# Banded attention on one Trainium2 core: two head pairs per round instead of one

## The chip, the cores and the metric

The kernel runs on one core of a Trainium2 chip. The metric is the device time of one execution in microseconds (us). The engines of the core work side by side: TensorE (PE in the rows, its weight loads PEld), VectorE (DVE), ScalarE (ACT), GpSimd (POOL), and SyncE (SP), which here only issues DMAs. Each engine runs its own instructions in order and waits on semaphores for the others.

## The reference, cut to what matters

Two blocks follow each other on 1024 tokens of width 1024. The second has three mixers; the change touches the third, attention within a band, and the order of the products that run beside it.

```python
def mixer_window_attention(q, k, v, gate, sink, bias, mask):
    # 8 query heads of 64, 2 key/value heads (4 query heads share one), blocks of 128 queries;
    # each block sees its own 128 keys, the 128 before and the 128 after
    s = jnp.einsum('bnqkgd,bnskd->bnkgqs', q, kb).astype(jnp.float32) * (HEAD_DIM_2 ** -0.5)
    s = jnp.where(mask[None, :, None, None], s + bias, NEG_INF_2)
    m = jnp.maximum(jnp.max(s, axis=-1, keepdims=True), sk)
    p = jnp.exp(s - m)
    p = p / (jnp.sum(p, axis=-1, keepdims=True) + jnp.exp(sk - m))
    o = jnp.einsum('bnkgqs,bnskd->bnqkgd', p.astype(vb.dtype), vb)
    return o.reshape(bsz, seq, W_C) * jax.nn.silu(gate)
# after the mixers: y = concat(ya, yb, yc) @ w_out;  x = layer_norm(ALPHA * x + y, ...)
```

## The kernel before, in words

All engines have programs written out by hand; nothing but the order of the calls and the semaphores sets the order of the work. The last stage but one is attention. Its unit is a **pair** `x` of 0 to 31 (`pair`, L362): two query heads of one block of 128 queries, `g` the key/value head (0 for x < 16), `n` the block, `p` which two of the four heads; `nb` is the number of key blocks in the band, 3, and 2 at both ends of the sequence (x = 0, 1, 14, 15, 16, 17, 30, 31).

Four kinds of work go to TensorE, each with its own shape in the array:

- `pair_scores(x)` (L1212, **S**): queries times keys, both heads at once in the two row halves of the array (64 rows by 128 columns), `nb*128` columns, into one bank of PSUM per head, banks 0 and 1. In the trace these are four records of L1220.
- `turn_p(x)` (L1223, **T**): `2*nb` transposes of the weights in the full array, banks 4 and 5, L1229.
- `weigh(x)` (L1233, **W**): the value products, the two heads in the two column halves (128 by 64), `4*nb` records of L1240, bank 6 or 7.
- `side(n, ks)` (L1244): a piece of one of the dense products that fill the time, in the full array with 512 columns each, three matmuls per step of k (L841, L842, L843), banks 2 and 3. For x < 16 a round takes three steps of k (9 matmuls; gates and queries of g = 1), for x >= 16 a whole tile of four steps (12 matmuls; the first half of the output product).

The loop at L1277 issues per round x: W(x-1), T(x), S(x+2), side. After it come 16 tiles of the output product (`tail`, L1291), with W(31) behind the first.

The other engines follow a pair in this way. DVE adds bias and takes the minimum of the negated scores (`pair_scores`, L1859, one custom instruction per head, L1869, into `sp[:, x % 2]`, which must have been transposed for x-2). ACT makes the exponentials and their sums in place (`weights`, L2346, L2352). DVE takes the reciprocal (`row_scale`, L1873), POOL multiplies both heads' rows by it (`scale_p`, L782, L787), TensorE transposes. ACT copies head 0 of the transposed weights out of bank 4 (`turned`, L2355, L2360), DVE head 1 out of bank 5 (`turned`, L1887, L1892), into the one buffer `pT`, which W(x-1) must have read. After W(x), DVE multiplies the product by the gate (`gate_out`, L1877, L1885). Between these stand on DVE and ACT the ends of the side products (`side_out`, dictionary `SIDE_OUT`, L375; for x >= 17 DVE adds the residual to the tile of the round before, L1907), and at `PIECE` (L373) the splitting of finished output features into a high and a low part (`high_y2` on ACT, L2310, `low_y2` on DVE, L1799). POOL also splits the coming weights into high and low parts, a quarter at a time (`split_part`, L762, L768 and L771): the first `W_Q1`, then the four chunks `W_O2` to `W_O2+3`. SP loads chunk `W_O2+3` (L600) when chunk `W_O2+2` has been split, and POOL splits it when side product 23 has left its buffers.

In PSUM a bank is taken with `take(b, name, value)` (L818): it waits for the semaphore that the bank's last user named.

```python
            for x in range(32):
                if x:
                    weigh(x - 1)
                if x == 16:
                    pe.wait_ge(s["v_y2lo"], 8)
                turn_p(x)
                if x + 2 < 32:
                    pair_scores(x + 2)
```

Of the kernel before, what the change touches and what calls it, by code (L numbers as in the profile page):

```python
# [7 lines left out]
F32 = mybir.dt.float32  # L8
# [98 lines left out]
def build(nc, I, out):  # L107
# [64 lines left out]
    with ctx:  # L172
# [3 lines left out]
        def region(kb4, *groups):  # L176

            found = []
            for group in groups:
                with ExitStack() as tmp:  # L180
                    found += [tmp.enter_context(nc.sbuf_tensor(n, s, t)) for n, s, t in group]
            sb(f"pad_{groups[0][0][0]}", [P, kb4])
            return found

        def sem(name):
# [4 lines left out]
        whi = [sb(f"whi{i}", [P, KT, CW], F32R) for i in range(2)]  # L190
        wlo = [sb(f"wlo{i}", [P, KT, CW], F32R) for i in range(2)]
        SL = KT * S
        (u_hi, u_lo, qT0, qT1, kt0, kt1, v0, v1, ST0, ST1, Wb, yt1, tmpj, smzb, h2, Q, y2a, _q, y2b, glu, _h, agb) = region(
            2 * SL,
            [("u_hi", [P, KT, S], F32R), ("u_lo", [P, KT, S], F32R)],
            [("qT0", [P, 2, S], F32), ("qT1", [P, 2, S], F32),
# [7 lines left out]
            [("y2a", [P, 4, 2, S], F32R), ("_q", [P, 2, NT * CW], F32), ("y2b", [P, 2, 2, S], F32R)],  # L204

            [("glu", [P, 2, GPAD], F32), ("_h", [P, 6 * S - 2 * GPAD - 4], F32), ("agb", [P, 2, S], F32)],
        )
        xr, yp_hi, um, ym_hi, x2_hi, res = region(
            SL, [("xr", [P, NT, D], F32)], [("yp_hi", [P, KT, S], F32R)], [("um", [P, KT, S], F32)],
            [("ym_hi", [P, KT, S], F32R)], [("x2_hi", [P, KT, S], F32R)], [("res", [P, NT, D], F32)])  # L210
        yp_lo, cc, ym_lo, x2_lo, y2c = region(
            SL, [("yp_lo", [P, KT, S], F32R)], [("cc", [P, KT, S], F32)],
            [("ym_lo", [P, KT, S], F32R)], [("x2_lo", [P, KT, S], F32R)], [("y2c", [P, 2, 2, S], F32R)])
        qTs, kts, vs, STs = (qT0, qT1), (kt0, kt1), (v0, v1), (ST0, ST1)

        pxhi, pxlo = yp_hi[:, 6:8, :], yp_lo[:, 6:8, :]
# [151 lines left out]
        def piece(i):  # L368

            g, hf, p = i // 4, i % 4 // 2, i % 2  # L370
            return g, hf, p, 16 * g + 8 * hf + 6 + p

        PIECE = {piece(i)[3] + 1: i for i in range(8)}  # L373

        SIDE_OUT = {0: 1, 3: 2, 6: 3, 8: 4, 11: 5, 14: 6, 16: 7}  # L375
        SIDE_OUT.update({17 + t: 8 + t for t in range(2 * NT)})
# [438 lines left out]
        def _(pe):  # L815
            last = {}

            def take(b, name, value):  # L818

                if b in last:  # L820
                    pe.wait_ge(s[last[b][0]], last[b][1])
                last[b] = (name, value)
                bank_of[name, value] = b
                return bank[b]
# [387 lines left out]
            def pair_scores(x):  # L1212
                g, n, p, lo, nb = pair(x)
                if x in (0, 1, 16, 17, 24, 25):
                    pe.wait_ge(s["a_q"], {0: 4, 1: 4, 16: 5, 17: 6, 24: 7, 25: 8}[x])
                for i in range(2):
                    ko = 64 * i
                    keys = kA if i == g else kB
                    ps = take(i, "v_s", 2 * x + i + 1)
                    pe.matmul(ps[:, 0:nb * P], qT2[ko:ko + 64, p, n * P:(n + 1) * P],  # L1220
                              keys[ko:ko + 64, lo * P:(lo + nb) * P], start=True, stop=True).then_inc(s["t_sc"], 1)

            def turn_p(x):  # L1223
                _, _, _, _, nb = pair(x)
                for i in range(2):
                    pe.wait_ge(s["g_nm"], 2 * x + i + 1)
                    ps = take(4 + i, ("a_pT", "v_pT")[i], x + 1)
                    for b in range(nb):
                        mm = pe.transpose(ps[:, b * P:(b + 1) * P],  # L1229
                                          sp[:, x % 2, i, BAND - (nb - b) * P:BAND - (nb - b - 1) * P], idn)  # L1230
                    mm.then_inc(s["t_pt"], 1)

            def weigh(x):  # L1233
                g, _, _, lo, nb = pair(x)
                ps = take(6 + x % 2, "v_o", x + 1)
                pe.wait_ge(s["a_pT"], x + 1)
                pe.wait_ge(s["v_pT"], x + 1)
                for b in range(nb):
                    for i in range(2):
                        mm = pe.matmul(ps[64 * i:64 * i + 64, 0:P], vt[:, lo + b, g * HD2:(g + 1) * HD2],  # L1240
                                       pT[:, i, b * P:(b + 1) * P], start=(b == 0), stop=(b == nb - 1))
                mm.then_inc(s["t_pv"], 1)

            def side(n, ks=range(KT)):  # L1244

                b = 2 + n % 2
                if n < 4:
                    w, i, name, value, hi, lo = W_CG1, n, "v_cg", n + 1, x2_hi, x2_lo
                elif n < 8:
                    w, i, name, value, hi, lo = W_Q1, n - 4, "a_q", n + 1, x2_hi, x2_lo  # L1250
                else:
                    w, i, name, value, hi, lo = W_O2 + (n - 8) // NT, n % NT, "v_r2", n - 7, y2_hi, y2_lo
                if ks[0] == 0:
                    side_bank[n] = take(b, name, value)
                group(w, i, hi, lo, name, value, ks=ks, ps=side_bank[n])
# [18 lines left out]
            side(0)  # L1274
            pair_scores(1)
            side(1)
            for x in range(32):  # L1277
                if x:
                    weigh(x - 1)
                if x == 16:  # L1280
                    pe.wait_ge(s["v_y2lo"], 8)
                turn_p(x)
                if x + 2 < 32:
                    pair_scores(x + 2)
                if x < 16:
                    for k in range(3 * x, 3 * x + 3):
                        side(2 + k // KT, range(k % KT, k % KT + 1))
                else:
                    side(8 + x - 16)

            def tail(i):  # L1291
                c, t = TAIL[i]
# [5 lines left out]

            for i in range(len(TAIL)):
                tail(i)  # L1300
                if i == 0:
                    weigh(31)

        def filled(eng, t_name, t_value, name, value):

# [5 lines left out]
        def _(ve):  # L1311
# [547 lines left out]
            def pair_scores(x):  # L1859
                g, n, p, _, nb = pair(x)  # L1860
                off = P if n == 0 else 0
                if n == 0:
                    ve.wait_ge(s[f"l_rb{p}"], 32 * (g + 1))
                for i in range(2):
                    ps = filled(ve, "t_sc", 2 * x + i + 1, "v_s", 2 * x + i + 1)
                    if x >= 2:
                        ve.wait_ge(s["t_pt"], 2 * x + i - 3)
                    h = 4 * g + 2 * p + i
                    ve.tensor_tensor_reduce(sp[:, x % 2, i, BAND - nb * P:BAND], ps[:, 0:nb * P],  # L1869
                                            rbias[:, 2 * p + i, off:off + nb * P], 1.0, nsink[:, h:h + 1],  # L1870
                                            ALU.add, ALU.min, nm[:, x % 2, i:i + 1]).then_inc(s["v_s"], 1)

            def row_scale(x):  # L1873
                ve.wait_ge(s["a_p"], 2 * x + 2)
                ve.reciprocal(rcx[:, x % 2, :], smx[:, x % 2, :]).then_inc(s["v_rc"], 1)  # L1875

            def gate_out(x):  # L1877
                g, n, p, _, _ = pair(x)
                if x == 0:
                    ve.wait_ge(s["a_f"], 12)  # L1880
                if x == 16:
                    ve.wait_ge(s["v_cg"], 4)
                ps = filled(ve, "t_pv", x + 1, "v_o", x + 1)
                y = gated[g][:, p, n * P:(n + 1) * P]
                ve.tensor_tensor(y, ps[:, 0:P], y, ALU.mult).then_inc(s["v_o"], 1)  # L1885

            def turned(x):  # L1887
                nb = pair(x)[4]
                ps = filled(ve, "t_pt", 2 * x + 2, "v_pT", x + 1)
                if x:  # L1890
                    ve.wait_ge(s["t_pv"], x)
                ve.tensor_copy(pT[:, 1, 0:nb * P], ps[:, 0:nb * P]).then_inc(s["v_pT"], 1)  # L1892

            def side_out(n):

# [23 lines left out]
            side_out(0)  # L1919
            for n in range(4, 8):  # L1920
                low_y2(n)
            for x in range(33):
                if x + 1 < 32:
                    row_scale(x + 1)
                if x:
                    gate_out(x - 1)
                if x < 32:
                    turned(x)
                if x + 2 < 32:
                    pair_scores(x + 2)  # L1930
                if x in SIDE_OUT:
                    side_out(SIDE_OUT[x])
                if x in PIECE:
                    low_y2(8 + PIECE[x])

            def final_norm(t):

# [31 lines left out]
        def _(ac):  # L1969
# [385 lines left out]
            def turned(x):  # L2355
                nb = pair(x)[4]
                ps = filled(ac, "t_pt", 2 * x + 1, "a_pT", x + 1)
                if x:
                    ac.wait_ge(s["t_pv"], x)
                ac.activation(pT[:, 0, 0:nb * P], ps[:, 0:nb * P], ACT.Copy).then_inc(s["a_pT"], 1)  # L2360

            def side_out(n):

# [14 lines left out]
            for x in range(33):  # L2378
                if x < 32:
                    turned(x)  # L2380
                if x in SIDE_OUT:
                    side_out(SIDE_OUT[x])
                if x + 2 < 32:
                    weights(x + 2)
                if x in PIECE:
                    high_y2(8 + PIECE[x])
            for t in range(NT):
                ac.wait_ge(s["v_lnv"], NH + NT + 2 + t + 1)
                root(sd[:, t:t + 1], v1_[:, t:t + 1])
# [29 lines left out]
```

## Time and profile before

| | |
|---|---|
| median of 3 runs | 1217.81 us (1216.48 to 1218.27) |
| the profiled execution's own time | 1219.74 us |
| its span in the trace | 1217.7 us |
| TensorE busy | 1183.7 us, 97% of the span |
| VectorE, GpSimd, ScalarE busy | 684.5, 450.1, 357.1 us |
| granted clock of TensorE, mean | 0.993 |

The span is the stretch that the trace covers, from the first instruction to the last; the own time has some 2 us around it. "Busy" counts the time in which an engine has an instruction in work. Start times in rows are us from the start of the span. Matmuls are pipelined, so that the records of neighbours overlap: the distance from one start to the next is what a matmul costs, and not its duration.

### The profile page before, as it was taken

The numbers are of one execution on the slowest core, as the hardware profiler recorded it, in microseconds if no ns is written. First come the engines' busy times: TensorE is split into PE (matmuls) and PEld (weight loads), VectorE is DVE, ScalarE is ACT, GpSimd is POOL, SyncE is SP. The second block draws the span as 40 slices with busy tenths as digits, with TensorE's granted clock in tenths as the row PEclk, the third lists the DMA queues.
The fourth block names the chain that finished last, engine by engine and source line by source line (L and its number), as shares of the span: only waits on it lengthen the run. The fifth ranks groups of instructions, "written<-read, shape, count | busy, mean of one in ns | idle before, by whom it ended". The sixth has DMA issues, their size and how long they took to land.

```text
span 1217.7 us, 15892 instructions
## 1 busy us (share of the span) xinstructions
PE 1183.7 (97%) x5921; PEld 953.9 (78%) x5921; DVE 684.5 (56%) x1242; ACT 357.1 (29%) x714; POOL 450.1 (37%) x431
## 2 busy tenths in 40 slices
PE   6999999999999999999998999999999999999995
PEld 5788888888888688787786788879888886666784
DVE  4545647342476303167767946856794524555468
ACT  6312121000012102546565511331111144443211
POOL 3324222232522322445665664203422315444343
PEclk9999999999999999999999999999999999999998
DMA  7141121453221222101114412232121110051102
GB/s 231 38 145 44 35 78 35 132 176 101 70 69 35 70 95 105 44 23 28 52 40 147 165 52 70 87 100 70 53 69 35 62 35 35 9 191 36 50 39 121
DMA packets 73884, 93.47 MB, mean 77 GB/s; under 512 B 13905, under 2 KB 53033, under 8 KB 73298
## 3 DMA queue, kind: packets, MB, share of 16 engines
q1 hardware_dynamic: 65090, 88.27, 21.6%
q10 hardware_dynamic: 8720, 4.20, 1.3%
q8 instruction: 48, 0.79, 0.3%
q14 instruction: 26, 0.21, 0.1%
HBM read 75.11 MB, written 18.92 MB: 77 GB/s over the span
## 4 chain that ended last, share of the span: by engine, by line
PE 86%; DVE 7%; POOL 2%; issue 2%; DMA 1%; ACT 1%; SPq 0%; ACTq 0%; POOLq 0%; DVEq 0%
PE bank L841 22%; PE bank L843 21%; PE bank L842 21%; PE bank L1066 3%; PE bank L1083 3%; PE bank L1220 2%; PE wide L1240 2%; PE wide L1229 2%; PE wide L1076 2%; DVE res L1943 1%; PE bank L1037 1%; PE bank L1026 1%; PE wide L841 1%; PE wide L843 1%; PE wide L842 1%
## 5 line engine op out<-in xcount | busy, mean ns | idle before, releaser
L622 POOL CAST whi<-wraw 128x2048 fp32r<-128x2048 f32 x31 | 58.9, 1900 | 463.1 <-PE bank L843 394.2
L841 PE MATMUL bank<-u_hi,wlo 128*128 128x512 f32 x512 | 201.2, 393 | 3.3 <-DVE u_lo L1338 3.3
L843 PE MATMUL bank<-u_hi,whi 128*128 128x512 f32 x512 | 199.8, 390 | 0.0
L842 PE MATMUL bank<-u_lo,whi 128*128 128x512 f32 x512 | 199.7, 390 | 0.0
L624 POOL TENSOR_TENSOR wlo<-wraw,whi 128x2048 fp32r<-128x2048 f32 x32 | 153.1, 4784 | 3.0 <-ACT whi L2252 0.5
L841 PE MATMUL bank<-x_hi,wlo 128*128 128x512 f32 x320 | 128.1, 400 | 0.8 <-issue 0.7
L843 PE MATMUL bank<-x_hi,whi 128*128 128x512 f32 x320 | 124.8, 390 | 0.0
L842 PE MATMUL bank<-x_lo,whi 128*128 128x512 f32 x320 | 124.8, 390 | 0.0
L841 PEld LDWEIGHTS bank<-u_hi,wlo 128*128 128x128 f32 x512 | 96.5, 189 | 25.6 <-DVE u_lo L1338 4.4
L843 PEld LDWEIGHTS bank<-u_hi,whi 128*128 128x128 f32 x512 | 96.4, 188 | 20.4
L842 PEld LDWEIGHTS bank<-u_lo,whi 128*128 128x128 f32 x512 | 96.6, 189 | 19.5
L841 PEld LDWEIGHTS bank<-x_hi,wlo 128*128 128x128 f32 x320 | 60.1, 188 | 21.7 <-issue 9.7
L787 POOL TENSOR_SCALAR sp<-sp,rcx 128x384 f32<-128x384 f32 (+1 forms) x64 | 36.1, 577 | 105.9 <-DVE rcx L1875 105.9
L843 PEld LDWEIGHTS bank<-x_hi,whi 128*128 128x128 f32 x320 | 60.1, 188 | 12.9
L1788 DVE SCALAR_TENSOR_TENSOR wide<-glu,VT,wide 128x1024 f32<-128x1024 f32 x58 | 69.3, 1280 | 0.0
L842 PEld LDWEIGHTS bank<-x_lo,whi 128*128 128x128 f32 x320 | 60.1, 188 | 11.4
L1083 PE MATMUL bank<-v,kwb 128*128 128x257 f32 x224 | 59.0, 386 | 1.1 <-DVE Cst L1588 0.9
L1066 PE MATMUL bank<-Cst,qT 128*128 128x257 f32 x224 | 58.1, 381 | 0.9 <-ACT tmpj L2174 0.8
L1465 DVE SCALAR_TENSOR_TENSOR cva<-um,VT,cva 128x1022 f32<-128x1022 f32 (+1 forms) x32 | 58.0, 1811 | 1.1
L2056 ACT ACTIVATE um<-bank 128x512 f32<-128x512 f32 x16 | 9.6, 599 | 155.7 <-PE bank L843 155.7
L710 POOL TENSOR_TENSOR Pm<-ST,Wb 128x128 f32<-128x128 f32 x64 | 30.3, 473 | 60.5 <-ACT Wb L2126 60.5
L1869 DVE CUSTOM_DVE_ANT_0 sp<-bank,rbias,nsink 128x384 f32<-128x384 f32 (+1 forms) x64 | 34.9, 582 | 29.4 <-PE bank L1220 29.1
(335 smaller groups left out, 2420.0 us busy)
## 6 DMA issues: line engine op xcount, KB each, us to landing
wraw<-in_w_in SPq DMA_DIRECT2D x27, 1024.0 KB, 5.3
wraw<-in_w_out SPq DMA_DIRECT2D x12, 1024.0 KB, 5.1
xr<-in_x SPq DMA_DIRECT2D x8, 512.0 KB, 8.4
hst<-in_x SPq DMA_DIRECT2D x4, 1024.0 KB, 5.1
hpool<-hst SPq DMA_DIRECT2D x4, 1024.0 KB, 4.1
smz<-mzs SPq DMA_DIRECT2D x16, 256.0 KB, 2.1
wraw<-nmax ACTq DMA_DIRECT2D x32, 128.0 KB, 3.0
h<-hpool SPq DMA_DIRECT2D x4, 1024.0 KB, 6.4
```

The costliest lines, as they stand in the source:

```text
L622: g_.tensor_copy(whi[w % 2][:, :, :], wraw[:, :, :]).then_inc(s["w_hi"], 1)
L624: g_.tensor_tensor(wlo[w % 2][:, :, :], wraw[:, :, :], whi[w % 2][:, :, :].bitcast(F32), ALU.subtract).then_inc(s["w_lo"], 1)
L710: g_.tensor_tensor(Pm[:, n % 2, :], STs[h % 2][:, ck, :], Wb[:, n % 2, :], ALU.mult).then_inc(s["g_P"], 1)
L787: g_.tensor_scalar(row, row, rcx[:, x % 2, i:i + 1], 0.5 if g else 1.0, ALU.mult, ALU.mult).then_inc(s["g_nm"], 1)
L841: pe.matmul(ps, al, bh, start=(k == 0), stop=False)
L842: pe.matmul(ps, ah, bl, start=False, stop=False)
L843: return pe.matmul(ps, ah, bh, start=False, stop=(k == nk - 1))
L1066: mm = pe.matmul(ps[:, 0:AUG], q[:, k, ck * P:(ck + 1) * P], Cst[:, d, k, :], start=(k == 0), stop=(k == 1))
L1083: mm = pe.matmul(ps[:, 0:AUG], kwb[:, m % 2, k * P:(k + 1) * P], v[:, ck, :], start=True, stop=True)
L1465: ins = ve.scalar_tensor_tensor(acc[:, a0:a1], um[:, j, a0 + sh:a1 + sh], tap(q), acc[:, a0:a1], ALU.mult, ALU.add)
L1788: ins = ve.scalar_tensor_tensor(dst, src, w, acc, ALU.mult, ALU.add)
L1869: ve.tensor_tensor_reduce(sp[:, x % 2, i, BAND - nb * P:BAND], ps[:, 0:nb * P], rbias[:, 2 * p + i, off:off + nb * P], 1.0, nsink[:, h:h + 1],
```

## The change

TensorE takes two pairs per round. With x0 even, a round is W(x0-2), W(x0-1), S(x0+2), S(x0+3), then T(x0) with its side products and T(x0+1) with its side products. W(30) and W(31) stand behind the last side product and ahead of the first tail tile. Every instruction stays what it was, in shape and number.

Banks are dealt out anew: S takes 0 and 1 for even x and 6 and 7 for odd x, W takes 4 (even) or 5 (odd), which T uses too. The transposed weights get a second buffer: even x use `pT`, odd x use `pTb` (x < 16) or `pTc`, which lie in parts of other regions that are free then, so that a copy of `turned(x)` waits for W(x-2) and no more for W(x-1). DVE's order becomes, per x0: `gate_out(x0-2)`, `gate_out(x0-1)`, `row_scale(x0+1)`, `turned(x0)`, `pair_scores(x0+2)`, `side_out(x0)`, two `low_y2` at x0 = 8, 16, 24, 32, `turned(x0+1)`, `row_scale(x0+2)`, `pair_scores(x0+3)`, `side_out(x0+1)`. ACT keeps its order, but for the two `high_y2`, which move. POOL and SP are unchanged.

```diff
+            [("_b", [P, 2 * SL - 2 * S], F32), ("pTb", [P, 2, S], F32)],
...
+            [("_c", [P, 2 * S], F32), ("pTc", [P, 2, S], F32)])
...
-        PIECE = {piece(i)[3] + 1: i for i in range(8)}
+        PIECES = {piece(i)[3] + 2: (i, i + 1) for i in range(0, 8, 2)}
+
+        def pT_of(x, i):
+            if x % 2 == 0:
+                return pT[:, i, :]
+            return (pTb if x < 16 else pTc)[:, i, HALF:HALF + BAND]
...
-                    ps = take(i, "v_s", 2 * x + i + 1)
+                    ps = take(6 * (x % 2) + i, "v_s", 2 * x + i + 1)
...
-                ps = take(6 + x % 2, "v_o", x + 1)
+                ps = take(4 + x % 2, "v_o", x + 1)
...
-                                       pT[:, i, b * P:(b + 1) * P], start=(b == 0), stop=(b == nb - 1))
+                                       pT_of(x, i)[:, b * P:(b + 1) * P], start=(b == 0), stop=(b == nb - 1))
...
-            for x in range(32):
-                if x:
-                    weigh(x - 1)
-                if x == 16:
+            for x0 in range(0, 32, 2):
+                if x0:
+                    weigh(x0 - 2)
+                    weigh(x0 - 1)
+                if x0 + 2 < 32:
+                    pair_scores(x0 + 2)
+                    pair_scores(x0 + 3)
+                if x0 == 16:
                     pe.wait_ge(s["v_y2lo"], 8)
-                turn_p(x)
-                if x + 2 < 32:
-                    pair_scores(x + 2)
-                if x < 16:
-                    for k in range(3 * x, 3 * x + 3):
-                        side(2 + k // KT, range(k % KT, k % KT + 1))
-                else:
-                    side(8 + x - 16)
+                for x in (x0, x0 + 1):
+                    turn_p(x)
+                    if x < 16:
+                        for k in range(3 * x, 3 * x + 3):
+                            side(2 + k // KT, range(k % KT, k % KT + 1))
+                    else:
+                        side(8 + x - 16)
+            weigh(30)
+            weigh(31)
...
             for i in range(len(TAIL)):
                 tail(i)
-                if i == 0:
-                    weigh(31)
...
-                if x:
-                    ve.wait_ge(s["t_pv"], x)
-                ve.tensor_copy(pT[:, 1, 0:nb * P], ps[:, 0:nb * P]).then_inc(s["v_pT"], 1)
+                if x >= 2:
+                    ve.wait_ge(s["t_pv"], x - 1)
+                ve.tensor_copy(pT_of(x, 1)[:, 0:nb * P], ps[:, 0:nb * P]).then_inc(s["v_pT"], 1)
...
-            for x in range(33):
-                if x + 1 < 32:
-                    row_scale(x + 1)
-                if x:
-                    gate_out(x - 1)
-                if x < 32:
-                    turned(x)
-                if x + 2 < 32:
-                    pair_scores(x + 2)
-                if x in SIDE_OUT:
-                    side_out(SIDE_OUT[x])
-                if x in PIECE:
-                    low_y2(8 + PIECE[x])
+            for x0 in range(0, 34, 2):
+                if x0:
+                    gate_out(x0 - 2)
+                    gate_out(x0 - 1)
+                if x0 < 32:
+                    row_scale(x0 + 1)
+                    turned(x0)
+                if x0 + 2 < 32:
+                    pair_scores(x0 + 2)
+                if x0 in SIDE_OUT:
+                    side_out(SIDE_OUT[x0])
+                for i in PIECES.get(x0, ()):
+                    low_y2(8 + i)
+                if x0 < 32:
+                    turned(x0 + 1)
+                if x0 + 2 < 32:
+                    row_scale(x0 + 2)
+                    pair_scores(x0 + 3)
+                if x0 + 1 in SIDE_OUT:
+                    side_out(SIDE_OUT[x0 + 1])
...
-                if x:
-                    ac.wait_ge(s["t_pv"], x)
-                ac.activation(pT[:, 0, 0:nb * P], ps[:, 0:nb * P], ACT.Copy).then_inc(s["a_pT"], 1)
+                if x >= 2:
+                    ac.wait_ge(s["t_pv"], x - 1)
+                ac.activation(pT_of(x, 0)[:, 0:nb * P], ps[:, 0:nb * P], ACT.Copy).then_inc(s["a_pT"], 1)
...
+                for i in PIECES.get(x, ()):
+                    high_y2(8 + i)
                 if x in SIDE_OUT:
                     side_out(SIDE_OUT[x])
                 if x + 2 < 32:
                     weights(x + 2)
-                if x in PIECE:
-                    high_y2(8 + PIECE[x])
```

## Rows read from the trace of the kernel before

**Rows 1.** The page: shares of the chain of waits that ended last, by engine.
```profile
PE 86%; DVE 7%; POOL 2%; issue 2%; DMA 1%; ACT 1%; SPq 0%; ACTq 0%; POOLq 0%; DVEq 0%
```

**Rows 2.** Busy time in stretches of attention; last come granted clock, DMA share, GB/s.
```profile
1005.40:1080.00 74.60, 74.60 (x482) 50.06 (x481) 37.07 (x120) 32.94 (x91) 34.34 (x67) 1.00 0.13 43
1080.00:1164.00 84.00, 84.00 (x519) 59.48 (x520) 42.28 (x121) 27.30 (x76) 35.40 (x60) 1.00 0.23 86
```

**Rows 3.** Timeline of TensorE, one round of x >= 16: start, duration, line, tiles.
```profile
1098.35 0.88 PE L1240 MATMUL wide<-pT,vt 128*64 128x128 f32 x12
1099.16 0.88 PE L1229 MATMUL wide<-cst,sp 128*128 128x128 f32 x6
1099.96 0.59 PE L1220 MATMUL bank<-kB,qT 64*128 64x384 f32 x1
...
1100.81 0.50 PE L841 MATMUL bank<-whi,y2a 128*128 128x512 f32 x1
1101.15 0.40 PE L842 MATMUL bank<-wlo,y2a 128*128 128x512 f32 x1
...
1103.43 0.39 PE L843 MATMUL bank<-whi,y2a 128*128 128x512 f32 x1
1103.75 0.88 PE L1240 MATMUL wide<-pT,vt 128*64 128x128 f32 x12
```

**Rows 4.** Timeline of TensorE, the same kinds in other neighbourhoods and sizes.
```profile
979.90 0.40 PE L843 MATMUL bank<-x_hi,whi 128*128 128x512 f32 x1
980.13 1.91 PE L1269 MATMUL wide<-cst,Q 128*128 128x128 f32 x16
981.80 0.47 PE L841 MATMUL bank<-x_hi,wlo 128*128 128x512 f32 x1
982.11 0.39 PE L842 MATMUL bank<-x_lo,whi 128*128 128x512 f32 x1
...
992.90 0.48 PE L1220 MATMUL bank<-kA,qT 64*128 64x256 f32 x1
...
993.22 0.38 PE L1220 MATMUL bank<-kA,qT 64*128 64x256 f32 x1
...
993.53 0.50 PE L841 MATMUL bank<-x_hi,wlo 128*128 128x512 f32 x1
...
1156.10 0.66 PE L1240 MATMUL wide<-pT,vt 128*64 128x128 f32 x8
1156.69 0.66 PE L1229 MATMUL wide<-cst,sp 128*128 128x128 f32 x4
1157.10 0.47 PE L841 MATMUL bank<-whi,y2a 128*128 128x512 f32 x1
```

**Rows 5.** Groups by line in 993 to 1170: busy, mean ns, idle before, releaser.
```profile
L2352 ACT ACTIVATE sp<-sp,nm 128x385 f32<-128x385 f32 x48 | 29.3, 614 | 30.6 <-DVE nm L1869 30.6
L1869 DVE CUSTOM_DVE_ANT_0 sp<-bank,rbias,nsink 128x384 f32<-128x384 f32 x48 | 27.7, 616 | 7.3 <-PE bank L1220 7.3
L787 POOL TENSOR_SCALAR sp<-sp,rcx 128x384 f32<-128x384 f32 x48 | 27.6, 588 | 65.3 <-DVE rcx L1875 65.3
...
L1892 DVE COPY pT<-wide 128x384 f32<-128x384 f32 x24 | 13.4, 558 | 11.8 <-PE wide L1229 11.8
...
L1907 DVE SCALAR_TENSOR_TENSOR res<-res,bank 128x512 f32<-128x512 f32 x16 | 10.9, 682 | 0.0
...
L1885 DVE TENSOR_TENSOR Q<-wide,Q 128x128 f32<-128x128 f32 x32 | 9.3, 290 | 36.8 <-PE wide L1240 36.8
```

**Rows 6.** Timelines of POOL, SP and DVE from the last pair into the tail.
```profile
1152.67 1.28 POOL L771 TENSOR_TENSOR wlo<-wraw,whi 128x512 fp32r<-128x512 f32 x1
1160.25 0.61 POOL L768 CAST whi<-wraw 128x512 fp32r<-128x512 f32 x1 [6.29 <-PE bank L843]
...
1153.98 0.38 SPq L395 DMA_DIRECT2D wraw<-in_w_out  x1
...
1179.51 3.13 DVE L1943 SCALAR_TENSOR_TENSOR res<-res,mv,pog 128x1024 f32<-128x1024 f32 x1
```

More of the change, by code:

```diff
@@ L192, in build @@
         SL = KT * S
-        (u_hi, u_lo, qT0, qT1, kt0, kt1, v0, v1, ST0, ST1, Wb, yt1, tmpj, smzb, h2, Q, y2a, _q, y2b, glu, _h, agb) = region(
+        (u_hi, u_lo, qT0, qT1, kt0, kt1, v0, v1, ST0, ST1, Wb, yt1, tmpj, smzb, h2, Q, y2a, _q, y2b, glu, _h, agb, _b, pTb) = region(
             2 * SL,
@@ L210, in build @@
             [("ym_hi", [P, KT, S], F32R)], [("x2_hi", [P, KT, S], F32R)], [("res", [P, NT, D], F32)])
-        yp_lo, cc, ym_lo, x2_lo, y2c = region(
+        yp_lo, cc, ym_lo, x2_lo, y2c, _c, pTc = region(
             SL, [("yp_lo", [P, KT, S], F32R)], [("cc", [P, KT, S], F32)],
-            [("ym_lo", [P, KT, S], F32R)], [("x2_lo", [P, KT, S], F32R)], [("y2c", [P, 2, 2, S], F32R)])
+            [("ym_lo", [P, KT, S], F32R)], [("x2_lo", [P, KT, S], F32R)], [("y2c", [P, 2, 2, S], F32R)],
+            [("_c", [P, 2 * S], F32), ("pTc", [P, 2, S], F32)])
         qTs, kts, vs, STs = (qT0, qT1), (kt0, kt1), (v0, v1), (ST0, ST1)
```

## The prediction, made before the change was run

> **What bounds the kernel now.** I read the page first. TensorE is busy for 97% of the span, and the chain of waits that ended last runs through it for 86% and through VectorE for 7% [rows 1]. Next the table of stretches: in attention TensorE is busy for all of 1005.4 to 1080 and of 1080 to 1164, at the full granted clock (1.00, the 2.4 GHz level), while DVE is at half, ACT at 30 to 45%, POOL at 45% [rows 2]. TensorE never runs dry there, so no engine or DMA beside it can give time back; only its own instruction stream can get shorter. The change removes no instruction. The question is therefore what TensorE pays where one kind of work follows another, and the timeline of TensorE shows that in the distances between starts.
>
> Within a side product matmuls start every 0.228 us (1101.15 to 1103.43 are ten) [rows 3]. Around the other kinds it takes longer. Bare lengths follow from two sizes of each: W takes 0.59 with 8 records and 0.81 with 12, so 0.22 per key block and 0.81 - 3 x 0.213 = 0.17 beside it; the six transposes of T before S take 0.80, sixteen alone take 1.67 (0.104 each), so 0.17 beside 0.63; S with 256 columns takes 0.63 and with 384 columns 0.85, so 0.21 beside 0.64 [rows 3, 4]. Of these 0.21, 0.11 lie between S's own two passes (0.32 apart at 256 columns, bare 0.21) and 0.10 behind it. The first side matmul after S takes 0.34 for 0.23 (0.11 more), and the last before W 0.32 for 0.23 (0.09 more) [rows 3]. So a round pays, beside bare work: side to W 0.09, W to T 0.17, T to S 0.17, inside S 0.11, S to side 0.21, in all 0.75 us of 5.40.
>
> What of this is a matter of changing the array's division? T and side both use the whole array: side to T costs 0.23 for 0.23 (979.90 to 980.13), nothing; T to side costs no gap (four transposes 0.41) and 0.08 on the first matmul (0.31 at 981.80) [rows 4]. These are the two neighbourhoods that the new order has instead.
>
> **The change, part by part.** Two rounds now hold eight borders: 1.50 us. Afterwards a double round has W W S S T side T side:
>
> - side to W 0.09, as now [rows 3].
> - W to W: same division, two banks. Not in the trace; nearest are the twelve records inside one W, which have no gap, and W to T at 0.17. I take 0, range 0 to 0.17.
> - W to S: from column halves to row halves, not in the trace; W to T and T to S both cost 0.17, side to W only 0.09. I take 0.17, range 0.09 to 0.21.
> - inside S and S to S: the first S has its 0.11; the second S may load its weights behind the first, so I take 0.05 for it, range 0 to 0.21 (0.11 inside it and 0.10 between them).
> - S to T: S to side costs 0.10 ahead of the first matmul and 0.11 on it; T's first load has its price in T to side. I take 0.10, range 0.05 to 0.21.
> - side to T 0, range 0 to 0.09; T to side 0.08, twice [rows 4], range 0.04 to 0.08.
>
> Sum 0.09 + 0 + 0.17 + 0.11 + 0.05 + 0.10 + 0 + 0.16 = 0.68, saved 1.50 - 0.68 = 0.82 us per double round. There are 14 full ones (x0 = 2 to 28): 11.5 us. The first (x = 0 and 1, no W of an earlier pair) had T to S twice, S twice, S to side twice, side to W and W to T, 1.24; it gets side to S 0.09, S 0.16, S to T 0.10 and T to side 0.16, 0.51: saved 0.7. The last (x = 30, 31 and W(31)) had side to W three times, W to T twice, T to side twice and W to side once (0.17 + 0.11): 1.05; it gets 0.79: saved 0.3. **Together 12.5 us.** Length of the key band does not enter: borders cost the same at two and three blocks [rows 3, 4].
>
> The Trainium skill, "TensorEngine Tiling (Array Packing)", Key Properties, says that a change of tiling mode, not a change of tile, drains TensorE. By that rule alone eight drains per two rounds become three, and at the mean 0.75 / 4 = 0.19 us of a border the saving would be 0.94 per double round, 14.1 over 15; the trace agrees that T beside side costs least, but shows 0.08 there and not 0.
>
> **What must hide, now that the cover moves.** I laid one double round of x >= 16 out, T(x0) at 0. TensorE: T to 0.64, side to 3.45, T(x0+1) to 4.1, side to 6.9, W W 7.0 to 8.45, S S to 9.95, T(x0+2) at 10.0. DVE, with 0.56, 2 x 0.54 to 0.62, 0.68 and 0.29 [rows 5]: `turned(x0)` 0.7 to 1.3, scores(x0+2) to 2.4, `side_out` to 3.1, `turned(x0+1)` 4.1 to 4.7, reciprocal, scores(x0+3) to 6.1, `side_out` to 6.8, `gate_out` at 7.7 and from 8.35 to 8.65. T and W now share banks 4 and 5: head 1 of T(x0+2) wants bank 5 at 10.3, so 1.7 us are spare. The reciprocal of x0+2 stands behind `turned(x0+1)`, which waits for T(x0+1); POOL's two products (0.59 each) still end at 6.1 for a T at 10.0: 3.9 spare. The reciprocal of x0+3 stands behind both `gate_out`, at 8.8; POOL ends at 10.0, T(x0+3) comes at 13.4: 3.4 spare. W(x0+1) wants the copies of 4.7 at 7.7. For x < 16 each side is 0.68 shorter, and all these stay above 1.5. The double `high_y2` and `low_y2` (about 0.6 and 0.7 us each, four times) delay the copies by under 1 us. The second `pT` buffer takes away the one wait that would have become tight. So I cost the moved waits at nothing.
>
> In the tail DVE becomes the pacer after the first tiles of c = 1 (3.13 us for one product beside POOL) [rows 6]. An earlier TensorE still moves it, since DVE cannot begin a tile before its product; the shift passes through if W(30), W(31) and tiles 0 to 3 come earlier by it and the weights for tile 4 are there. That chain gets tighter: the load of chunk W_O2+3 was issued at 1153.98, landed some 5.1 us later, and POOL could begin its split at 1160.25, when side 23 ended [rows 6]. Now `scale_p(31)` and with it the end of the split before come some 2 us later against T(30). Counted from T(30): load issued 3.2, landed 8.3, split over (four parts of about 2 us) at 16.4; tile 4 wants it at 7.7 + 4 x 2.73 = 18.6. Spare 2.2 us.
>
> The profiled execution took 1219.74 us, its span 1217.7. 1219.74 - 12.5 = 1207.2 for an execution like it; the median of the runs shown lies 1.9 lower, at 1217.8, which gives **1205.3 us**.
>
> **Rivals.**
>
> 1. *The price hangs on the group and not on the change of shape.* Then W to W costs 0.17, S to S 0.21 with its inside, S to T 0.21. Against my sum that is 0.17 + 0.16 + 0.11 = 0.44 more, 6.6 over 15, so 1211.9. For it: no W W or S S stands in the trace. Against: side to T at 0, and twelve records of W without a gap [rows 4].
> 2. *The rule of drains holds in full:* a border inside one division is free and every other costs about 0.19. Saved 14.1: 1203.7. For it: side to T 0. Against: 0.08 at T to side.
> 3. *Slower: DVE comes late to banks 4 and 5.* Place: `gate_out(x0+1)` to T(x0+2), head 1, where only S S (1.5 us) lies between the end of W and the transposes. It decides from 1.7 us of lateness on; to be slower than before it must be later than 1.7 + 12.5 / 15 = 2.5 us in every double round, and at 3.5 us it would give 1217.8 + 15 x 1.0 = 1233. Against: DVE is busy for half of the stretch [rows 2] and free a full microsecond before W(x0) ends.
> 4. *The tail keeps part of it:* the split of W_O2+3 comes later than I think (the load shares the DMA engines, POOL is slowed beside DVE) and tile 4 waits 1 to 5 us: about 1208 to 1210.
> 5. *No change:* TensorE's borders are short only because of something that the new order does not keep, and the new ones cost as much: 1217.
>
> **How the numbers follow.** Forecast 0.60; rival 1 0.14; rival 2 0.12; rival 3 0.05, of it half slower than before and half a small gain lost; rival 4 0.06; rival 5 0.03. The unknown prices at their low ends give 0.09 + 0 + 0.09 + 0.11 + 0 + 0.05 + 0 + 0.08 = 0.42, saved 16.1, 1201.7; all at their high ends give 0.09 + 0.17 + 0.21 + 0.11 + 0.21 + 0.21 + 0.09 + 0.16 = 1.25, saved 3.7, 1214.1. Not all fall to one side; the range runs from 1203.0 to 1212.5 and leaves out the slow rivals and the far ends. Two measurements of this kernel can be told apart from about 0.2%, 2.4 us. Faster by more: the forecast, rivals 1, 2, 4 and some of 3: 0.92. Within it: 0.04. Slower: 0.04.
>
> **What would show it.** In the profile after, TensorE stays busy for all of attention, the count of records is the same, and a double round of x >= 16 is some 10.0 us long, where two rounds were 10.8; one of x < 16 some 8.6 for 9.45. Between starts: W x12 to the next W 0.64, W to S 0.81, S to S about 0.7, S to T 0.74, T to side 0.64, side to T 0.23. The first tail tile starts 12 to 13 us earlier but for W(31), now ahead of it, and the end of the span follows. I am wrong if S S takes 1.7 us and W W 1.6 (rival 1), if T's loads show idle time released by DVE's `gate_out` or by POOL (rival 3), or if tile 4 shows a wait for `wlo` (rival 4).

## The result, and the profile after

| | before | after |
|---|---|---|
| median of the runs | 1217.81 us (4 runs) | 1204.20 us (4 runs, 1202.67 to 1204.65) |
| profiled execution, own time | 1219.74 us | 1204.48 us |
| span | 1217.7 us | 1202.5 us |

The ratio is 0.9889, with a 95% interval of 0.9876 to 0.9901: 13.6 us less, where 12.5 were forecast.

First the stretches of attention in the kernel after (columns as in [rows 2]). TensorE is still never idle to speak of: 74.60 of 74.60, then 69.89 of 70.00. What it got rid of was inside "busy".

```profile
1005.40:1080.00 74.60, 74.60 (x528) 56.93 (x528) 38.63 (x134) 35.58 (x101) 36.39 (x70) 1.00 0.26 90
1080.00:1150.00 70.00, 69.89 (x470) 54.91 (x469) 38.42 (x109) 25.42 (x67) 31.72 (x54) 1.00 0.15 53
```

The two profiled executions do not differ by attention alone: the one before came later to its first scores (992.90 [rows 4]) than the one after (991.21). So I compare attention by itself, from the first record of S(0) to DVE's addition of the fifth tail tile, from which on DVE sets the pace. The rows are from the timelines: the fifth addition of the kernel before, then the first scores and the fifth addition of the kernel after.

```profile
1174.60 0.69 DVE L1959 TENSOR_TENSOR res<-res,bank 128x512 f32<-128x512 f32 x1 [1.30 <-PE bank L843]
```
```profile
991.21 0.48 PE L1228 MATMUL bank<-kA,qT 64*128 64x256 f32 x1
...
1159.37 0.69 DVE L1977 TENSOR_TENSOR res<-res,bank 128x512 f32<-128x512 f32 x1 [1.30 <-PE bank L851]
```

Before, 1174.60 - 992.90 = 181.70 us; after, 168.16. **Attention lost 13.5 us.** The other 1.7 of the two spans' difference lie ahead of it, where the programs are the same, and do not belong to the change; the medians, 13.6 apart, agree with 13.5.

One double round after, for x >= 16, from TensorE's timeline (compare [rows 3]). L1248 is W, L1228 S, L1237 T, L849 to L851 are side.

```profile
1096.99 0.88 PE L1248 MATMUL wide<-pT,vt 128*64 128x128 f32 x12
1097.69 0.83 PE L1248 MATMUL wide<-pTc,vt 128*64 128x128 f32 x12
1098.45 0.59 PE L1228 MATMUL bank<-kB,qT 64*128 64x384 f32 x1
...
1098.88 0.48 PE L1228 MATMUL bank<-kB,qT 64*128 64x384 f32 x1
...
1099.20 0.48 PE L1228 MATMUL wide<-kB,qT 64*128 64x384 f32 x1
...
1099.52 0.48 PE L1228 MATMUL wide<-kB,qT 64*128 64x384 f32 x1
...
1099.94 0.88 PE L1237 MATMUL wide<-cst,sp 128*128 128x128 f32 x6
1100.57 0.48 PE L849 MATMUL bank<-whi,y2a 128*128 128x512 f32 x1
1100.89 0.40 PE L850 MATMUL bank<-wlo,y2a 128*128 128x512 f32 x1
...
1103.16 0.39 PE L851 MATMUL bank<-whi,y2a 128*128 128x512 f32 x1
1103.39 0.82 PE L1237 MATMUL wide<-cst,sp 128*128 128x128 f32 x6
1103.96 0.48 PE L849 MATMUL bank<-whi,y2a 128*128 128x512 f32 x1
1104.28 0.40 PE L850 MATMUL bank<-wlo,y2a 128*128 128x512 f32 x1
...
1106.56 0.39 PE L851 MATMUL bank<-whi,y2a 128*128 128x512 f32 x1
1106.87 0.88 PE L1248 MATMUL wide<-pT,vt 128*64 128x128 f32 x12
```

From 1096.99 to 1106.87 are 9.88 us, where two rounds were 10.81 (5.40 for one, 1098.35 to 1103.75; two in a row take 10.81). For x < 16 a double round takes 8.52 (two starts of W, below); two rounds there were 9.45.

```profile
1018.61 0.88 PE L1248 MATMUL wide<-pT,vt 128*64 128x128 f32 x12
...
1027.13 0.88 PE L1248 MATMUL wide<-pT,vt 128*64 128x128 f32 x12
```

Now what each border (the place where one kind of work follows another) costs beside the bare lengths of the prediction: side to W 0.09 (0.31 for 0.23); W W up to the start of S 1.46 for 1.28, so 0.18; inside the first S 0.11 (0.43 for 0.32); the second S 0 (its passes 0.32 apart, and 0.32 behind the first S); S to T 0.10 (0.42 for 0.32); T to side 0.63, then 0.32 on the first matmul, 0.08 together; side to T 0 (0.23); the second T takes only 0.57, so that T and first matmul have 0.02. Sum 0.58, where 0.68 was forecast and 1.50 was paid before.

### The profile page after: what moved, and what is told of

It is laid out like the page before. It is cut to its first block, busy times and chain, and to the rows that moved or that the text cites. A ratio compares the mean times of both kernels' runs of the same rounds, so it can differ in the third digit from the quotient of the medians.

```text
span 1202.5 us, 15890 instructions
## 1 busy us (share of the span) xinstructions
PE 1168.2 (97%) x5921; PEld 954.2 (79%) x5921; DVE 680.1 (57%) x1242; ACT 355.9 (30%) x714; POOL 450.2 (37%) x431
## 4 chain that ended last, share of the span: by engine, by line
PE 87%; DVE 8%; POOL 2%; issue 2%; DMA 1%; ACT 1%; SPq 0%; ACTq 0%; POOLq 0%; DVEq 0%
PE bank L849 21%; PE bank L851 21%; PE bank L850 21%; PE bank L1074 3%; PE bank L1091 3%; PE wide L1237 2%; PE wide L1248 2%; PE wide L1084 2%; DVE res L1961 1%; PE bank L1034 1%; PE bank L1228 1%; PE bank L1045 1%; PE wide L851 1%; PE wide L850 1%; PE wide L849 1%
## 5 line engine op out<-in xcount | busy, mean ns | idle before, releaser
L849 PE MATMUL bank<-u_hi,wlo 128*128 128x512 f32 x512 | 201.1, 393 | 3.4 <-DVE u_lo L1349 3.3
L851 PE MATMUL bank<-u_hi,whi 128*128 128x512 f32 x512 | 199.9, 390 | 0.0
L849 PE MATMUL bank<-x_hi,wlo 128*128 128x512 f32 x320 | 127.7, 399 | 0.8 <-issue 0.7
L851 PE MATMUL bank<-x_hi,whi 128*128 128x512 f32 x320 | 124.8, 390 | 0.0
L849 PEld LDWEIGHTS bank<-u_hi,wlo 128*128 128x128 f32 x512 | 96.4, 188 | 26.0 <-DVE u_lo L1349 4.5
L851 PEld LDWEIGHTS bank<-u_hi,whi 128*128 128x128 f32 x512 | 96.5, 189 | 20.2
L849 PEld LDWEIGHTS bank<-x_hi,wlo 128*128 128x128 f32 x320 | 60.1, 188 | 13.8 <-issue 1.9
L851 PEld LDWEIGHTS bank<-x_hi,whi 128*128 128x128 f32 x320 | 60.1, 188 | 12.8
L849 PE MATMUL bank<-whi,ym_lo 128*128 128x512 f32 x128 | 50.2, 392 | 0.2 <-ACT tmpj L2192 0.2
```

The costliest lines, as they stand in the source:

```text
L849: pe.matmul(ps, al, bh, start=(k == 0), stop=False)
L851: return pe.matmul(ps, ah, bh, start=False, stop=(k == nk - 1))
```

## The experiments

Two theories stood against each other. **Borders**: the gain is what TensorE no longer pays where its array is divided anew. **Slack**: the gain comes from the second buffer, the new banks and DVE's new order. For each run I also give attention's length, measured as above. A double round is the work of two pairs; in the orders with one pair per round it is two rounds.

**S ahead of T, in the kernel before, nothing else.**

```diff
-                turn_p(x)
                 if x + 2 < 32:
                     pair_scores(x + 2)
+                turn_p(x)
                 if x < 16:
```

> The kernel before with one pair per round, one pT buffer and the old banks and DVE order; only S(x+2) moves ahead of T(x), so a round is W S T side. Border theory (the price is paid where the array's division changes, and T beside side is nearly free): side to W 0.09, W to S 0.17, inside S 0.11, S to T 0.10, T to side 0.08 = 0.55 per round where it was 0.75; 29 rounds and a bit, 5.9 us less than before: about 1211.9. Rival that the gain came with the second buffer and the new order on DVE (slack, not borders): no change, 1217.8. Rival that each group carries its own price whatever stands beside it: no change either.

Measured: 1212.15 us, ratio 0.9957 (0.9944 to 0.9969); attention 176.15, 5.55 less than before (5.9 were expected). One buffer, old banks, old DVE order: slack is not what gave this. A round from its timeline (here L1240 is W, L1220 S, L1229 T):

```profile
1103.11 0.88 PE L1240 MATMUL wide<-pT,vt 128*64 128x128 f32 x12
1103.91 0.59 PE L1220 MATMUL bank<-kB,qT 64*128 64x384 f32 x1
...
1104.76 0.87 PE L1229 MATMUL wide<-cst,sp 128*128 128x128 f32 x6
...
1108.33 0.88 PE L1240 MATMUL wide<-pT,vt 128*64 128x128 f32 x12
```

5.22 us for the 5.40 of [rows 3]. W to S costs the 0.17 that W to T cost (0.80 from start to start, 0.81 there); the saving is that T now stands beside side, and S no more.

**Only the W's side by side.** The changed kernel with the scores behind each T, S in banks 0 and 1, W in 6 and 7 (the two lines with the banks are left out here):

```diff
-                if x0 + 2 < 32:
-                    pair_scores(x0 + 2)
-                    pair_scores(x0 + 3)
...
                 for x in (x0, x0 + 1):
                     turn_p(x)
+                    if x + 2 < 32:
+                        pair_scores(x + 2)
```

> The changed kernel with the scores put back behind each T: W W, then T S side twice; S in banks 0 and 1, W in 6 and 7. Only W's are side by side. Border theory with the prices of the rows: 0.09 + 0.17 + 2 x (0.17 + 0.11 + 0.21) = 1.24 per double round for 1.50 before: 3.9 us less than before, about 1213.9. If only the number of changes of division counts, at 0.19 each, six for eight: 5.6 us less, 1212.2. Slack theory (buffers and DVE's order are what gains): as fast as the changed kernel, 1204.

Measured: 1213.36 us, ratio 0.9964 (0.9952 to 0.9977); attention 177.30, 4.4 less than before. The second buffer and DVE's whole new order are in it (the new banks are not), and two thirds of the gain are missing. Slack falls here a second time. The row prices (3.9) and the count at 0.19 (5.6) miss the 4.4 by 0.5 and 1.2 us. A T behind side starts S 0.75 later and not 0.80, which saves 0.05 more per double round than the row prices have:

```profile
1108.30 0.82 PE L1237 MATMUL wide<-cst,sp 128*128 128x128 f32 x6
1109.05 0.59 PE L1228 MATMUL bank<-kB,qT 64*128 64x384 f32 x1
```

But for x >= 16 the double round took 10.58 for 10.81 (two starts of W) and saved only 0.23, less than the 0.26 of the row prices:

```profile
1102.30 0.88 PE L1248 MATMUL wide<-pT,vt 128*64 128x128 f32 x12
...
1112.88 0.88 PE L1248 MATMUL wide<-pT,vt 128*64 128x128 f32 x12
```

A side product took up to 0.03 us longer here than in the kernel before (2.32 for 2.29 from its second to its twelfth matmul), for a reason that no run shows. For x < 16 the saving was 0.29 (9.16 for 9.45). The first and the last double round gave 0.3 each, where the estimate had counted the two as one; most of the 0.5 lies there.

**The two scores apart.** W W, then S T side twice, with banks, buffers and DVE's order of the changed kernel:

```diff
-                if x0 + 2 < 32:
-                    pair_scores(x0 + 2)
-                    pair_scores(x0 + 3)
...
                 for x in (x0, x0 + 1):
+                    if x + 2 < 32:
+                        pair_scores(x + 2)
                     turn_p(x)
```

> The changed kernel with the two scores apart: W W, then S T side twice. Border theory with the prices seen after: 0.09 + 0.18 + 0.11 + 0.10 + 0.08 + 0.09 + 0.11 + 0.10 + 0.08 = 0.84 per double round for 0.58 in the changed kernel, 14 times: 3.6 us more than it, about 1207.8. Only the number of changes of division, 0.19 each, five for three: 5.3 us more, 1209.5. Slack theory: no change from 1204.2, since banks, buffers and DVE's order stay.

Measured: 1209.59 us, ratio to before 0.9933 (0.9920 to 0.9945); attention 173.44, 5.3 more than the changed kernel. The nine prices in that expectation were added up wrongly: they make 0.94, not 0.84, and so 0.36 per double round and 5.0 us in 14, which is near what was measured. One double round took 10.25 us (two starts of W):

```profile
1099.38 0.88 PE L1248 MATMUL wide<-pT,vt 128*64 128x128 f32 x12
...
1109.63 0.88 PE L1248 MATMUL wide<-pT,vt 128*64 128x128 f32 x12
```

This run is the third order of the same instructions in which TensorE is as busy as ever (for all of the 74.60 us from 1005.40 to 1080.00 in each of the three). With the first it parts the gain: S ahead of T 5.5 us, then W beside W 2.7 (176.15 to 173.44; buffers, banks and DVE's order change in this step too), then S beside S 5.3 (173.44 to 168.16, where nothing but the order on TensorE changes), together 13.5.

**DVE's old order under the new order of TensorE.** The loop of `gate_out`, `turned` and the rest as before, one pair at a time, `gate_out(x - 1)` ahead of `turned(x)`:

```diff
-            for x0 in range(0, 34, 2):
...
+            for x in range(33):
+                if x + 1 < 32:
+                    row_scale(x + 1)
+                if x:
+                    gate_out(x - 1)
+                if x < 32:
+                    turned(x)
+                if x + 2 < 32:
+                    pair_scores(x + 2)
```

> The changed kernel with DVE's old order, one pair at a time: gate_out(x0) stands ahead of turned(x0+1). W(x0+1) then waits for W(x0) to end, gate_out (0.29) and the copy (0.56) with their handoffs: some 0.95 us per double round in which TensorE is idle, 15 times 14 us; and gate_out(x0+1) stands behind the reciprocal of x0+3, so that head 1 of T(x0+2) may wait for bank 5, up to 0.5 us more. Expected 1218 to 1226: all of the gain gone or more. If TensorE's stream were covered by slack on DVE as it was before, nothing would change: 1204.

Measured: 1224.81 us, ratio 1.0056 (1.0040 to 1.0071), slower than before; attention 189.26, 21 more than the changed kernel. TensorE, from the timeline:

```profile
1108.33 0.88 PE L1248 MATMUL wide<-pT,vt 128*64 128x128 f32 x12
1110.16 0.88 PE L1248 MATMUL wide<-pTc,vt 128*64 128x128 f32 x12 [0.95 <-DVE pTc L1903]
```

The second W comes 1.83 us after the first, not 0.70: the 0.95 of the expectation and 0.18 beside it. There are 16 such waits, one in each pair of W, and the longer distances between the two W make 17.6 of the 21 us. DVE's timeline shows the cause, the product with the gate (L1896) ahead of the copy (L1903):

```profile
1098.13 0.29 DVE L1896 TENSOR_TENSOR Q<-wide,Q 128x128 f32<-128x128 f32 x1 [4.32 <-PE wide L1248]
1098.33 0.55 DVE L1903 COPY pTc<-wide 128x384 f32<-128x384 f32 x1
```

Another 2.2 us are lost at T(30). It waited for a `gate_out` too, so that its first side matmul came 1.33 us behind its start and not 0.72 (0.6 us more). Behind this wait the granted clock fell: its mean over the next 3.6 us is 0.53 (columns as in [rows 2], the clock is the last but two), which is near the 1.2 GHz level, and side matmuls start 0.43 us apart and not 0.23 (1.6 us more). Just before, TensorE had stood idle for 0.95 us at W(29) and for 0.73 at T(30).

```profile
1156.28 0.46 PE L1237 MATMUL wide<-cst,sp 128*128 128x128 f32 x2 [0.73 <-DVE Q L1896]
...
1157.39 0.63 PE L851 MATMUL bank<-whi,y2a 128*128 128x512 f32 x1
1157.82 0.63 PE L849 MATMUL bank<-whi,y2a 128*128 128x512 f32 x1
```
```profile
1156.40:1160.00 3.60, 3.60 (x11) 2.84 (x11) 1.02 (x2) 0.00 (x0) 2.40 (x4) 0.53 0.04 8
```

The last 1.3 us, some 0.1 per double round, are not assigned. So DVE's new order shows no gain of its own in any run and is yet a condition: without it the change loses.

**W W straight ahead of T.** S S moved ahead of W W, so that nothing covers the banks which W and T share:

```diff
-                if x0:
-                    weigh(x0 - 2)
-                    weigh(x0 - 1)
                 if x0 + 2 < 32:
                     pair_scores(x0 + 2)
                     pair_scores(x0 + 3)
+                if x0:
+                    weigh(x0 - 2)
+                    weigh(x0 - 1)
```

> The changed kernel with S S ahead of W W, so that T(x0+2) follows W(x0+1) at once and the shared banks 4 and 5 have no cover but head 0 of T. Same number of borders (0.58 within 0.05). In the changed kernel the last double round, which has no S, shows 0.52 us from T(30)'s start to head 1 where 0.21 are work: 0.31 of waiting for gate_out; with three key blocks head 0 lasts 0.11 longer, so 0.2 per double round, 3 us in all: about 1207.3. If the banks cost nothing (DVE always in time): 1204.2. If gate_out's place behind other work on DVE mattered, it would be 0.5 or more each, 1212 and up.

Measured: 1208.03 us, ratio to before 0.9923 (0.9910 to 0.9937); attention 171.69, 3.5 more than the changed kernel. The wait is there, in T's weight loads: three, then a gap for which the profile names no releaser, then three more, 0.52 from the first start where three transposes are 0.31. A double round of x >= 16 took 10.14 us for 9.88; this wait is 0.2 of the difference.

```profile
1102.26 0.31 PEld L1237 LDWEIGHTS wide<-cst,sp 128*128 128x128 f32 x3 [0.17 <-issue]
1102.78 0.31 PEld L1237 LDWEIGHTS wide<-cst,sp 128*128 128x128 f32 x3 [0.22 <-issue]
```

**Other banks for the last four W.**

```diff
-                ps = take(4 + x % 2, "v_o", x + 1)
+                ps = take((4 if x < 28 else 6) + x % 2, "v_o", x + 1)
```

> The changed kernel with W(28) to W(31) in banks 6 and 7, which are free by then. T(30) no longer waits for bank 5: its four transposes to the first side matmul take 0.41 us as before and not 0.72; 0.3 us off the span, far below what a timing can tell. If the gap at T(30) is no bank wait but POOL's product for head 1, it stays.

Measured once, 1204.97 us, which tells nothing at this size. Attention took 167.86, 0.3 less. First T(30) in the changed kernel, then with other banks:

```profile
1137.57 0.96 PE L1237 MATMUL wide<-cst,sp 128*128 128x128 f32 x4
1138.29 0.47 PE L849 MATMUL bank<-whi,y2a 128*128 128x512 f32 x1
```
```profile
1138.30 0.66 PE L1237 MATMUL wide<-cst,sp 128*128 128x128 f32 x4
1138.71 0.47 PE L849 MATMUL bank<-whi,y2a 128*128 128x512 f32 x1
```

0.72 became 0.41. The edit changed nothing but the bank, so the bank was the wait. This is the version with the shortest attention, by an amount that no timing of mine confirms.

## Why the prediction was right

- *What bounds.* TensorE's own stream did, and inside "busy". The three reorderings of the same instructions, at 1212.2, 1213.4 and 1209.6, show that by themselves.
- *The sum.* The full double round was forecast to save 0.82 us and saved 0.92 (10.81 to 9.88, 9.45 to 8.52). Side to W, inside S and S to T were priced right to 0.01. W W and W to S were right as a sum only, 1.46 for 1.45: W W is 0.70 between starts, not 0.64, and W to S 0.76, not 0.81. Two terms were mis-sized, both upward: the second S, taken at 0.05, cost 0; T to side was taken at 0.08 twice, but costs 0.08 only behind S, and 0.02 where T itself stands behind side (0.57 to the side start, 0.32 for the first matmul). By the starts of W in the timelines the 14 full double rounds saved 12.7 us where 11.5 were forecast, the first 0.8 for 0.7, and the last nothing for 0.3. So the forecast of 12.5 missed the measured 13.6 by 1.1 us with errors of both signs; that the unforeseen loss in the last double round makes the miss smaller is luck.
- *What I missed.* This is the 0.3 of the last double round, where no S stands between W(29) and T(30). The shared bank, rated at 1.7 us of spare by its S S, has none there, and T(30) waits 0.3 us. The run with S S moved away makes that wait general: 0.2 us in each double round, most of its 3.5 us.
- *Waits costed at nothing.* DVE's `gate_out` were forecast at 0.7 and 1.35 us after the start of W W, and came at 0.92 and 1.58 (timeline below). The second ended at 1098.86, 1.4 us before head 1 of T wants the bank (0.31 behind T's start at 1099.94); 1.7 were forecast. Of DVE's order I had laid out the hand-offs but did not say what the order was for; the run with the old one priced it at 21 us.

```profile
1097.91 0.29 DVE L1896 TENSOR_TENSOR Q<-wide,Q 128x128 f32<-128x128 f32 x1 [1.26 <-PE wide L1248]
1098.57 0.29 DVE L1896 TENSOR_TENSOR Q<-wide,Q 128x128 f32<-128x128 f32 x1 [0.36 <-PE wide L1248]
```

- *The tail.* The chain got tighter as forecast: POOL now waits for the load and not for TensorE (timelines of POOL, SP and TensorE below). The load was issued at 1141.04 and the split began at 1146.14, 5.1 us on; it ended at 1154.70, and tile 4 wanted it at 1156.45. Spare 1.7 us, forecast 2.2; the four parts took 8.6 us where about 8 were assumed.

```profile
1146.14 0.61 POOL L776 CAST whi<-wraw 128x512 fp32r<-128x512 f32 x1 [5.13 <-DMA wraw<-in_w_out]
...
1153.41 1.29 POOL L779 TENSOR_TENSOR wlo<-wraw,whi 128x512 fp32r<-128x512 f32 x1
```
```profile
1141.04 0.38 SPq L403 DMA_DIRECT2D wraw<-in_w_out  x1
```
```profile
1156.45 0.39 PE L849 MATMUL bank<-whi,y2b 128*128 128x512 f32 x1
```

- *Rivals.* The first (price on the group) fell: S S took 1.49 us and W W 1.46, where it wanted 1.7 and 1.6. The second (only changes of division cost, about 0.19 each) forecast 14.1 us and comes nearer than my sum (12.5) to the 13.6 measured, so that the prices of single borders did no better on the total than a plain count. Per double round the orders make 8 changes (before), 6 (S ahead of T), 6 (W W alone), 5 (S apart), 3 (after), and attention took 181.7, 176.2, 177.3, 173.4, 168.2: at 13.5 / (15 x 5) = 0.18 each, the middle ones come out at 176.3, 176.3 and 173.6. The Trainium skill, "TensorEngine Tiling (Array Packing)", Key Properties, has that rule (a change of mode drains, a change of tile does not); the runs agree with it as a count, but for 1 us in the order with W W alone. The order with W straight ahead of T has 3 changes too; its 171.7 us less 15 waits of 0.2 are 168.7. The third, DVE late to the banks, did not come; a neighbour of it, DVE late with the copy, came as soon as DVE's order was undone, and ended where that rival ends, slower than before. The fourth, the tail, stayed away by 1.7 us. The fifth, no change, fell with the total.

## What to carry to other kernels

Where TensorE is busy all the time, look at the distances between starts where one kind of matmul follows another: here each change between the whole array, its row halves and its column halves cost about 0.18 us, and a new order of the calls took five of eight away. Count such changes per round and try the cheapest reordering first. Swapping two lines gave 5.5 of the 13.5 us without a buffer. When groups are doubled, write down for each engine what the second member waits for; a product that may be late must not stand ahead of a copy that the next matmul needs.

## What the runs showed of the hardware that I had not expected

The price of transposes depends on what stands ahead of them: six of them take 0.63 us behind scores and 0.57 behind a side product. The weight loads of the changed kernel show the difference. Behind scores the first load starts with the first transpose (1099.94). Behind a side product it starts 0.22 us before T (1103.39), while the last side matmul is in work, and T follows that matmul by 0.23, as one side matmul follows another.

```profile
1099.94 0.64 PEld L1237 LDWEIGHTS wide<-cst,sp 128*128 128x128 f32 x6 [0.55 <-POOL sp L795]
1103.17 0.80 PEld L1237 LDWEIGHTS wide<-cst,sp 128*128 128x128 f32 x6
```

A stall costs more than its length, in two ways. In the run with DVE's old order the wait was 0.95 us, but the distance between the two W grew by 1.13. The other 0.18 are as much as a border costs elsewhere; that the second W pays one anew after standing still is my reading, and no run takes it apart. And at T(30), where two waits (0.95 and 0.73 us) fell within 3 us, the granted clock went down and cost another 1.6 us. In the double rounds of that run with the one wait alone no side matmuls start 0.43 apart.
